# Retention's value projection: four weight units at once for three and a half of its four token tiles

## The reference

```python
proj = h @ w_in                       # h: 512 x 1024, w_in: 1024 x 6144
q, k, v, g = jnp.split(proj, [RET_QK_WIDTH, 2 * RET_QK_WIDTH, 2 * RET_QK_WIDTH + RET_WIDTH], axis=-1)
q = apply_rope(q, cos, sin)
k = apply_rope(k, cos, sin) * (RET_QK_DIM ** -0.5)
scores = jnp.einsum('bhncd,bhnkd->bhnck', qc, kc) * intra_decay[:, None]
o_intra = jnp.einsum('bhnck,bhnke->bhnce', scores, vc)
o = rms_norm_f32(o, gn_g.reshape(RET_HEADS, RET_V_DIM))
o = o.reshape(B, S, RET_WIDTH) * jax.nn.silu(g.astype(jnp.float32))
return o.astype(h.dtype) @ w_out
```

## Time and profile before

| what | value |
|---|---|
| runs shown | 1814.16, 1814.34, 1816.74 us; median 1814.34 |
| the profiled execution | 1818.31 us |
| its span, first to last instruction | 1816.5 us |
| mean granted TensorE clock | 0.992 of 2.4 GHz |
| matmul busy | 1769.1 us |
| instructions | 25949 |
| weights and the rest read | 169.69 MB |

### The profile page before, as it was taken

One profiled execution on the slowest core, in us unless ns is written; L12 is line 12 of the kernel. 1 busy time (PEld: TensorE's weight loads), 2 busy tenths in 40 slices (PEclk: granted clock), 3 DMA queues, 4 the chain that ended last, 5 costly groups with the idle time before them and its releaser, 6 DMA issues.

```text
span 1816.5 us, 25949 instructions
## 1 busy us (share of the span) xinstructions
PE 1769.1 (97%) x9150; PEld 1471.2 (81%) x9150; DVE 902.9 (50%) x1470; ACT 471.1 (26%) x950; POOL 1104.5 (61%) x848
## 2 busy tenths in 40 slices
PE   6999999999999999999999999989999999999998
PEld 4888888888888888888878778877978878888887
DVE  4754726474344434453343698797373563213311
ACT  4121221200232223222221227554332422002200
POOL 3656555689364544555457668974066588767863
PEclk9999999999899999999999999999999999999999
DMA  9533222285233223322223332200023233333331
GB/s 347 169 87 93 75 81 75 87 298 164 69 93 88 79 64 91 92 80 75 63 87 93 95 85 59 71 24 24 24 70 88 76 104 93 104 101 86 103 97 55
DMA packets 281588, 172.87 MB, mean 95 GB/s; under 512 B 6000, under 2 KB 272560, under 8 KB 280496
## 3 DMA queue, kind: packets, MB, share of 16 engines
q1 hardware_dynamic: 275024, 151.01, 28.3%
q10 hardware_dynamic: 6496, 20.93, 3.3%
HBM read 169.69 MB, written 2.10 MB: 95 GB/s over the span
## 4 chain that ended last, share of the span: by engine, by line
PE 89%; DVE 5%; SPq 2%; DMA 1%; issue 1%; POOL 1%; ACT 1%; POOLq 0%; DVEq 0%; ACTq 0%
PE acc L386 14%; PE acc L388 14%; PE acc L387 14%; PE ob L386 4%; PE ob L387 4%; PE ob L388 4%; PE acc L416 3%; PE acc L418 3%; PE acc L417 3%; PE sc L1624 2%; PE acc L434 2%; PE sc L1604 2%; PE acc L435 2%; PE acc L436 2%; SPq L670 1%
## 5 line engine op out<-in xcount | busy, mean ns | idle before, releaser
L762 POOL TENSOR_TENSOR wl<-raw,wh 128x512 fp32r<-128x512 f32 x456 | 641.0, 1426 | 19.4
L759 POOL TENSOR_SCALAR wh<-raw 128x1024 fp32r<-128x1024 f32 (+1 forms) x232 | 267.6, 1154 | 584.8 <-PE acc L388 156.2
L386 PE MATMUL acc<-hh,wh 128*128 128x512 f32 x800 | 325.5, 407 | 1.2 <-ACT sq L1405 1.2
L388 PE MATMUL acc<-hh,wl 128*128 128x512 f32 x800 | 313.5, 392 | 0.0
L387 PE MATMUL acc<-hl,wh 128*128 128x512 f32 x800 | 312.7, 391 | 0.0
L386 PEld LDWEIGHTS acc<-hh,wh 128*128 128x128 f32 x800 | 151.1, 189 | 35.4 <-issue 2.7
L388 PEld LDWEIGHTS acc<-hh,wl 128*128 128x128 f32 x800 | 150.8, 189 | 33.1
L387 PEld LDWEIGHTS acc<-hl,wh 128*128 128x128 f32 x800 | 151.3, 189 | 32.3 <-issue 2.4
L386 PE MATMUL acc<-Yh,wh 128*128 128x512 f32 x256 | 100.7, 393 | 0.0
L386 PE MATMUL ob<-Yh,wh 128*128 128x512 f32 x256 | 100.5, 393 | 0.0
L388 PE MATMUL ob<-Yh,wl 128*128 128x512 f32 x256 | 99.7, 390 | 0.0
(11 more groups left out here) (522 smaller groups left out, 3648.2 us busy)
## 6 DMA issues: line engine op xcount, KB each, us to landing
raw<-in_att_w_in SPq DMA_DIRECT2D x64, 512.0 KB, 3.9
raw<-in_mlp_w SPq DMA_DIRECT2D x64, 512.0 KB, 3.9
raw<-in_ret_w_in SPq DMA_DIRECT2D x48, 512.0 KB, 3.7
ada_w<-in_ada_w ACTq DMA_DIRECT2D x8, 1536.0 KB, 6.9
raw<-in_w_in SPq DMA_DIRECT2D x23, 512.0 KB, 3.6
ada_w<-in_ada_w SPq DMA_DIRECT2D x16, 512.0 KB, 9.3
raw<-in_ret_w_out SPq DMA_DIRECT2D x16, 512.0 KB, 4.2
raw<-in_att_w_out SPq DMA_DIRECT2D x16, 512.0 KB, 4.0
```

The lines of the kernel that those rows point to most:

```text
L386: e.matmul(bank[:, :], wh[:, s, k, :], rhs_high(k), start=(start and k == 0), stop=False)
L388: last = e.matmul(bank[:, :], wl[:, s, k, :], rhs_high(k), start=False, stop=(stop and k == k1 - 1))
L759: e.tensor_scalar(wh[:, s, 0:k1, :], raw[:, s, 0:k1, :], 1.0, 1.0, ALU.mult, ALU.mult).then_inc(high_done, 1)
L762: low = e.tensor_tensor(wl[:, s, k0:k0 + KT // 2, :], raw[:, s, k0:k0 + KT // 2, :], wh[:, s, k0:k0 + KT // 2, :].bitcast(F32), ALU.subtract)
```

## The change

In ret_values, token tile 2 comes first, with all four units, and its own order of passes: for all eight k it streams the high part of the units against hh and hl (16 matmuls), and only then waits for the low parts and streams these (8 matmuls). It begins when the fourth high part is there (high_done, u + 4); before, the first two units had to be split in full. Tile 3 follows as before, then tile 0, now with all four units at once, then tile 1, still in two halves of two units. Units 0 and 1 are given back at the end of the first half of tile 1, units 2 and 3 at its end. Tile 3 gets a step of its own (r_v3), for which ScalarE waits in place of the counter. The number of columns streamed stays the same; per head 96 matmuls of 256 columns and 48 of 512 become 48 and 72.

```diff
                 for t in (2, 3, 0, 1):
-                    if t % 2 == 0:
+                    if t != 1:
                         e.wait_ge(*PE.at(f"r_v{t}", i))
                     else:
-                        e.wait_ge(unit_used, c + 6 if t == 3 else c + 8)
+                        e.wait_ge(unit_used, c + 8)
...
-                e.wait_ge(split_done, u + 2)
-                for t in range(2):
-                    e.wait_ge(*AC.at(f"r_qk{t}", i))
-                    tile(t, acc[t], 0, 2)
-                e.wait_ge(split_done, u + 4)
+                def high_first(t, bank, u):
+                    o = bank[:, :].rearrange("p (a n) -> p a n", a=4)
+                    for k in range(KT):
+                        e.matmul(o, hh[:, k, t * P:(t + 1) * P], wh[:, s0:s0 + 4, k, :], start=(k == 0), stop=False)
+                        e.matmul(o, hl[:, k, t * P:(t + 1) * P], wh[:, s0:s0 + 4, k, :], start=False, stop=False)
+                    e.wait_ge(split_done, u + 4)
+                    for k in range(KT):
+                        last = e.matmul(o, hh[:, k, t * P:(t + 1) * P], wl[:, s0:s0 + 4, k, :], start=False, stop=(k == KT - 1))
+                    return last
+
+                e.wait_ge(high_done, u + 4)
                 e.wait_ge(*AC.at("r_qk2", i))
-                tile(2, ob[0], 0, 4).then_inc(*PE.done("r_v2"))
+                high_first(2, ob[0], u).then_inc(*PE.done("r_v2"))
                 e.wait_ge(*AC.at("r_qk3", i))
-                tile(3, ob[1], 0, 4).then_inc(unit_used, 2)
-                tile(0, acc[0], 2, 2).then_inc(*PE.done("r_v0"))
+                tile(3, ob[1], 0, 4).then_inc(*PE.done("r_v3"))
+                e.wait_ge(*AC.at("r_qk0", i))
+                tile(0, acc[0], 0, 4).then_inc(*PE.done("r_v0"))
+                e.wait_ge(*AC.at("r_qk1", i))
+                tile(1, acc[1], 0, 2).then_inc(unit_used, 2)
                 tile(1, acc[1], 2, 2).then_inc(unit_used, 2)
```

## The result

The changed kernel takes 1830.04 us (median of 5 runs, 1825.07 to 1831.72), the kernel before 1816.35 us (median of 5, 1814.16 to 1816.86). The ratio is 1.0068, with a 95% interval of 1.0056 to 1.0080: slower by 10 to 14.5 us, 12.4 in the middle. The forecast was +11.4 us. In absolute time it was 1825.7 us with a range of 1821.5 to 1829.5, worked from a median of 1814.34 us for three runs of the kernel before. The median of its five runs is 2.0 us higher, and 1830.04 lies 0.5 us above that range. As a difference from the kernel before the range is +7.2 to +15.2 us, and the two measured medians are 13.7 us apart. The profiled execution took 1830.61 us for a span of 1828.8; before, 1818.31 and 1816.5.

The account below looks back on a forecast made before the run. TensorE, busy for 97% of the span, was taken to bound the kernel. Heads 1 to 3 (+6.0), head 0 (+2.1) and clock falls (+3.3) gave +11.4 on a median of 1814.34: 1825.7 us, range 1821.5 to 1829.5.

Parts of the forecast that it names:

- (a): Value projection of head 1 before the change: 23.38 us from k1's end, its wait included.
- (c): Value projection after the change: 22.18 us of TensorE work without waits.
- (b): Token tile 0 of the projection: 24 matmuls of 512 columns replace 48 of 256, saving 0.31 us.
- (d): Ahead of the projection: TensorE waits 3.22 us, uncovered, for GpSimd's fourth high half.
- (e): Old low-half wait, 0.86 us start to start, goes; low halves inside tile 2 cost nothing, 0.3 to 0.4 us spare.
- (f): Sum for each of heads 1 to 3: 25.40 against 23.38 us, +2.0 each, +6.0 for three.
- (g): Head 0: wait of 4.33 us, projection 26.51 against 24.40 us, +2.1; load and split unaffected by the change.
- (h): Slots 0 and 1 given back 5.0 us later; gate units still in time with 3 and 5 us spare, costing nothing.
- (i): Banks, ScalarE's evictions and VectorE's rope around the projection: no cost.
- (j): Clock falls to half behind two of the four new waits, 1.65 us each, +3.3 us; bounds 0 and 11.2.
- The rival with three or four falls, or longer ones: Clock falls behind three or four of the projection waits, or for longer: 1827.4 to 1830.4 us; chance 0.22.
- The faster rival: Fourth high half ready at 140.0 with faster splits, wait 0.2 us, four heads gain 1.0 us each: 1810.3 us; chance 0.02.

Follow-up runs that it names:

- e2: Changed kernel with the first half of token tile 1 moved ahead of the high-half wait, units 0 and 1 given back after tile 0; 1813.04 us, ratio 0.9986.
- e3: Kernel before's order, half tiles of tiles 0 and 1 first, with only tile 2's high passes first taken from the change; 1813.35 us, ratio 0.9986.
- e4: e2 without the high passes first, so tile 2 waits for all four low halves; 1832.27 us, ratio 1.0089.
- the three executions: Changed kernel, unedited, profiled three times: 1830.61, 1828.23 and 1829.10 us.
- The two executions of the kernel before: Kernel before, unedited, profiled twice: 1818.31 and 1818.71 us.
- e6: Kernel before with units 0 and 1 given back only at the projection's very end, tile 3 with its own step; 1816.77 us, ratio 1.0002.
- e1: Changed kernel with 12 throwaway 512-column matmuls per head ahead of the wait for the fourth high half; 1824.27 us, ratio 1.0045.
- e5: Changed kernel with VectorE's rope done on only 8 of 512 token columns; 1819.38 us, ratio 1.0022.
- The first execution: First profiled run of the changed kernel, unedited; 1830.61 us.
- the two others: Second and third profiled runs of the changed kernel, unedited; 1828.23 and 1829.10 us.
- the second execution of before: Second profiled run of the kernel before, unedited; 1818.71 us.
- the third execution: Third profiled run of the changed kernel, unedited; 1829.10 us.

## Why the prediction was right, point by point

**The mechanism was right, the closeness of the number is partly luck.** The uncovered wait for the fourth high half and the falls of the clock behind it are what the runs show. Head 0, the size of the falls and the step to the median were mis-sized, and their errors partly cancel.

**What bounds the kernel, (a) and (c): right.** A projection without wait and without fall was to be 22.18 us; head 2 of the changed kernel has 249.88 - 227.68 = 22.20.

**(b) The wide tile 0: right by its rows.** 0.31 us were forecast from the pitches, and e2 beside e3 shows 0.3. The Trainium skill's gap rule ("TensorE: Matmul & The Clock Gate", Back-to-back issue gap) would have it at 0.06; here the measurement decides against it. The same section gives the formula for an isolated matmul and states about 131 ns at 512 columns for a stream with weight loads; this case's stream has 226.7 ns and bears out neither.

**(d), (e), (f) The new wait: right.** 3.22 us forecast from k1's end to the projection, 144.62 - 141.43 = 3.19 measured; the fourth high split starts 143.01 - 141.43 = 1.58 us behind k1's end, where it was 1.62 (the prediction set its sign of being wrong at 1.6, a line drawn too near to the 1.62); no wait inside tile 2; a head's loss at full clock +2.0 forecast and 2.02 in head 2. e4 shows the low half's wait where nothing covers it.

**(g) Head 0: the mechanism was right, the size off.** 4.33 us of wait were forecast and 61.45 - 59.46 = 2.0 measured. The step that failed is that the third split starts at 58.04, when its load has landed, and that the load doesn't depend on what the change moves. Its issue stays in the same place in SyncE's queue, but in the changed kernel it lands sooner: GpSimd's third split starts at 56.25, 55.95 and 56.90 in the three executions, in the first two without waiting for the load. The two executions of the kernel before have 58.04 and 57.52, and e6, with the same matmuls in the same order, has 57.79; e1 to e5, each with another order of the projection, have 55.87 to 56.85. Three late and eight early starts without overlap are more than the scatter between executions, and why the load lands sooner stays open. The wait is then 2.0, 2.0 and 3.0 us, and at full clock head 0 takes 24.2, 24.2 and 25.2 us, level with the 24.40 of before or 0.8 above, not 2.1.

**(h), (i) Release, banks, evictions: right.** GpSimd's first gate split starts 165.82 - 141.43 = 24.4 us behind k1's end, where it was 157.93 - 139.94 = 18.0: 6.4 later, 5.0 as forecast and 1.5 from the fall; no wait of TensorE for it, and e6 shows the release alone at 1.0002.

**(j) The clock: right in kind, mis-sized in two terms that partly cancel.** Falls were forecast behind two of four waits, at 1.65 us each, 3.3 in all. The first execution has three falls worth 1.7, 1.5 and 2.8, 6.0 in all; the two others have two falls each, worth 4.4 and 4.3 together. So the number of falls, two to three, was near, but the price was not always that of the row taken: three of the six falls behind the 3.2 us waits last longer and cost 2.7 to 2.8 us, which the prediction held as its upper bound. e1 against the changed kernel gives 4 to 6 us for the same thing. Head 0's 1.3 to 2.3 us too many and the falls' 1 to 3 us too few cancel, which is luck, and why +11.4 stands beside 12.4. The rival with three or four falls, or longer ones (1827.4 to 1830.4), describes the falls as well as the forecast does: the first execution has three, and each of the three has a long one. The Trainium skill's rule ("TensorE: Matmul & The Clock Gate", Why this matters for your kernels), to leave no gaps over about 3 us, is borne out in direction: filling the gap removed all the falls. As a threshold it is not: head 2 of the first execution kept its clock behind 3.04 us, and the second execution of before lost it behind 2.22 us.

**From the sum to the median: mis-sized.** The forecast put the median 4.0 us under the profiled execution, from three runs of the kernel before. With five runs the distance is 1818.31 - 1816.35 = 2.0 us, and for the changed kernel it is 1830.61 - 1830.04 = 0.6. This is what took 1830.04 beyond the absolute range.

**The faster rival left out a step.** It let the fourth high half end at 140.0, as though the split could start before k1 was used up. e5 took the backlog away and found the wait at 1.5 us: above the 1.20 us from which the change would gain. With this order of work faster splits alone would not have made the change a gain.

**Not settled:** what in an execution decides whether an idle stretch of 2 to 3 us brings the clock down. The runs show that it differs between executions and that neither the place nor the chip decides it alone. Also open: why the third unit's load of head 0 lands sooner in the changed kernel.

## What to carry to other kernels

When a ring's last slot is freed by the very instruction that stands ahead of its user, the wait of its user can't be taken away by splitting faster (1.5 us of it stayed in e5): put work that needs only the earlier slots between the two. Here one half tile of 2.9 us ahead of a 3.2 us wait turned a loss of 12 us into a gain of 3. Price an uncovered wait of a few microseconds on TensorE at about twice its length in the worst case (3.2 us of wait and 2.8 of half clock in head 3), since the clock may fall behind it; the same wait filled with throwaway matmuls was cheaper than left idle.

## What the hardware did that was not expected

Useless work made the kernel faster: 48 throwaway matmuls in e1 took 5 to 6 us off the changed kernel. Behind the same 3.03 or 3.04 us of idle time a fall of the clock cost 1.5 us in head 1 and 2.8 us in head 3 of one execution, and nothing in head 2. And idle stretches of 1.83 us (head 0 of the changed kernel: a fall in the first execution, none in the second) and 2.22 us were enough for a fall in one execution and not in another, while 2.79 us (head 0 in the third execution) brought none.
